# Two-layer decoder step on eight cores: windowed attention rebuilt with queries in the partitions and a true row maximum

## What is computed

```python
def sink_attention(q, k, v, mask, sinks):
    s = jnp.einsum('bnqhgd,bnkhd->bnhgqk', q, k, ...) * (SWA_HEAD_DIM ** -0.5)
    s = jnp.where(mask[None, :, None, None, :, :], s, NEG_INF)
    sink = sinks.astype(jnp.float32).reshape(SWA_KV_HEADS, SWA_GROUP)[None, None, :, :, None, None]
    m = jnp.maximum(jnp.max(s, axis=-1, keepdims=True), sink)
    p = jnp.exp(s - m)
    p = p / (jnp.sum(p, axis=-1, keepdims=True) + jnp.exp(sink - m))
    return jnp.einsum('bnhgqk,bnkhd->bnqhgd', p.astype(v.dtype), v)
```

## Time and profile before

| | us |
|---|---|
| median of 3 runs (lowest to highest) | 2911.85 (2911.38 to 2926.31) |
| span of the profiled execution, slowest core | 2913.1 |
| spans of the 8 cores | 2885.2 to 2913.1 |
| TensorE busy | 2194.7 (75%) |
| VectorE busy | 1130.9 (39%) |
| ScalarE busy | 895.0 (31%) |
| GpSimd busy (DMA issues) | 257.3 (9%) |

### The profile page before, as it was taken

The page is one execution under the profiler, slowest core; times in us unless marked ns, Lnnn a source line. Parts: engine busy times, 40 slices in busy tenths (PEclk is TensorE's granted clock), DMA queues, the critical chain, the costliest instruction groups (busy, mean ns, idle before and its releaser), DMA issues.

```text
span 2913.1 us, 36426 instructions; the slowest of 8 cores (2885.2 to 2913.1 us)
## 1 busy us (share of the span) xinstructions
PE 2194.7 (75%) x11759; PEld 1031.3 (35%) x11759; DVE 1130.9 (39%) x2050; ACT 895.0 (31%) x1678; POOL 257.3 (9%) x311
## 2 busy tenths in 40 slices
PE   4768876987789868887798689776654499762697
PEld 1323333433334343333243434333211245341353
DVE  4542127136431172265311631645345331271422
ACT  2441134114521251144211520445233221343211
POOL 0000100110001100100011001000111201000010
PEclk9889988998879999999798999898755689895698
DMA  9547881797549827974488369544787878625274
GB/s 197 81 60 101 122 125 30 102 141 149 86 60 138 130 36 108 145 152 73 73 116 129 46 102 139 100 73 77 205 292 264 235 112 127 98 32 111 43 113 97
DMA packets 293096, 336.42 MB, mean 115 GB/s; under 512 B 7184, under 2 KB 257808, under 8 KB 292752
## 3 DMA queue, kind: packets, MB, share of 16 engines
q0 software_dynamic: 256944, 272.89, 59.4%
q1 hardware_dynamic: 35968, 61.20, 6.8%
HBM read 528.55 MB, written 46.79 MB: 198 GB/s over the span
## 4 chain that ended last, share of the span: by engine, by line
PE 60%; DVE 14%; DMA 11%; issue 8%; ACT 6%; DVEq 1%; SPq 0%; ACTq 0%; POOL 0%; POOLq 0%
PE pb L415 59%; DMA wr<-w 5%; DVE arena L424 4%; DVE arena L433 4%; DMA arena<-st_in 4%; ACT arena L421 3%; DVE rstd L433 2%; ACT sq L421 1%; ACT L421 1%; PE pb L418 1%; DVE hT L427 1%; DMA xT<-xTp 1%; DVE arena L427 1%; DVE stat L594 1%; DMA wr<-wo 1%
## 5 line engine op out<-in xcount | busy, mean ns | idle before, releaser
L415 PE MATMUL pb<-hT,wr 128*128 128x512 bf16 x3776 | 911.9, 399 | 81.5 <-DVE hT L427 68.3
L415 PEld LDWEIGHTS pb<-hT,wr 128*128 128x128 bf16 x3776 | 379.4, 101 | 592.2 <-issue 202.9
L415 PE MATMUL pb<-arena,wr 128*128 128x512 bf16 (+1 forms) x2720 | 535.7, 362 | 47.3 <-DMA wr<-w 21.8
L421 ACT ACTIVATE arena<-pb 128x512 bf16<-128x512 f32 (+3 forms) x584 | 319.9, 559 | 718.1 <-PE pb L415 629.4
L415 PEld LDWEIGHTS pb<-arena,wr 128*128 128x128 bf16 x2720 | 255.6, 103 | 323.6 <-issue 84.9
L415 PE MATMUL pb<-arena 128*128 128x128 bf16 (+2 forms) x576 | 146.4, 358 | 277.8 <-DVE arena L424 151.7
L424 DVE TENSOR_TENSOR arena<-arena,pb 128x512 bf16<-128x512 f32 x220 | 133.7, 608 | 526.4 <-PE pb L415 505.3
L436 POOL DMA_DIRECT2D wr<-w x144 | 125.0, 869 | 1350.7 <-PE pb L415 1349.1
L421 ACT ACTIVATE sq<-xT 128x512 bf16<-128x512 f32 x160 | 93.2, 622 | 491.2 <-PE pb L415 335.2
L415 PE MATMUL pb<-wr,hT 128*128 128x512 bf16 x1024 | 234.1, 389 | 0.0
L424 DVE TENSOR_TENSOR xT<-pb,xT 128x512 f32<-128x512 f32 x96 | 66.4, 692 | 419.9 <-PE pb L415 419.9
(11 more groups left out here) (79 smaller groups left out, 1623.0 us busy)
## 6 DMA issues: line engine op xcount, KB each, us to landing
wr<-w POOLq DMA_DIRECT2D x112, 1024.0 KB, 12.2
arena<-st_in SPq DMA_DIRECT2D x64, 512.0 KB, 8.0
srs<-arena POOLq DMA_DIRECT2D x64, 512.0 KB, 7.9
wr<-wo POOLq DMA_DIRECT2D x30, 1024.0 KB, 9.6
wr<-wqk POOLq DMA_DIRECT2D x16, 1024.0 KB, 13.3
wr<-wv POOLq DMA_DIRECT2D x16, 1024.0 KB, 11.7
wr<-wg POOLq DMA_DIRECT2D x16, 1024.0 KB, 9.9
wr<-w POOLq DMA_DIRECT2D x16, 768.0 KB, 13.6
```

The source lines that it names most:

```text
L415: S.op("pe", lambda e: e.matmul(out, lhsT, rhs, start=start, stop=stop), r, w)
L421: S.op("act", lambda e: e.activation(out=out, in_=in_, func=func, bias=bias, scale=scale), r, w)
```

## The change

- Weights: the unit `kz` is gone. The query columns and the rows of `wo1` are reordered so that head j of key head 0 sits in partitions 0 to 63 and head j of key head 1 in 64 to 127 of one chunk. Keys are projected once into `kT1` (8 matmuls of 512 columns); values are projected directly with positions in the partitions (`pb<-wr,hT`, 4 times 8 matmuls of 128 columns) and a bias add on VectorE.
- Prompt attention runs over 16 quads a tile (block, four heads). `q_scores(i)`: for each key head a 512-column matmul of the identity with the additive mask, then four 256-column score matmuls with 64 rows; VectorE takes two row maxima (128 by 2 rows of 256) and two 128x4 operations; ScalarE four exponentials of 128x256 with a bias from memory and a row sum, and a 128x4 exponential. `q_norm(i)`: VectorE adds and inverts 128x4, GpSimd scales 4 times 128x256. `q_out(i)`: 8 transposes of the probabilities; for odd i a copy of 128x1024 from PSUM on ScalarE and one on VectorE, four matmuls of 512 columns and 64 output rows (`arena,v`), and a 128x512 copy on ScalarE.
- Samples: the cached keys and values come in two DMAs of 1 MB on GpSimd's queue, in front of the load of `kv`; keys are transposed 8 at a time into `KcT`; four quads, each with four sequences, through the same three functions.

```diff
-                plan += [("q1", 0), ("q1", 1), ("kz",), ("kv",), ("wo1", 0), ("wo1", 1)]
+                plan += [("q1", 0), ("q1", 1), ("kv",), ("wo1", 0), ("wo1", 1)]
...
+                dma("pool", Kc[:, :, :], ck.rearrange("b k c -> k b c"), [], [Kcb], "kc")
+                dma("pool", Vc[:, :, :], cv.rearrange("b k c -> k b c"), [], [Vcb], "vc")
...
+            for blk in range(nblk):
...
+                    mm(bk[:, c0:256], cx.hT[:, kc, cs], wu[:, kc, c0:256], kc == 0, kc == KC - 1, [wub, cx.hb[kc]], [bb])
...
+            if sample:
+                for g in range(2):
...
+                    act(KcT[:, g * 8:(g + 1) * 8, :], tbv.rearrange("p (b k) -> p b k", b=8), AF.Copy, [tbb], [KcTb[g]])
...
+            def q_scores(i):
...
+                                mm(bks[kvh][0][:, :], ident_bf, cb[:, CB_MPR:CB_MPR + 512], True, False, [cbb], [bks[kvh][1]])
+                    for u in range(2):
+                        for kvh in range(2):
+                            rows = slice(kvh * 64, (kvh + 1) * 64)
+                            bk, bb, _ = bks[kvh]
+                            mm(bk[:, u * 256:u * 256 + w_], qT1[rows, 2 * jp + u, qs], kT1[rows, blk * 128 + k0:blk * 128 + 256], False, u == 1,
+                               [kT1b[blk + 1], kT1b[blk], qT1b[2 * jp + u]], [bb])
+                    for kvh in range(2):
+                        bk, bb, _ = bks[kvh]
+                        rmax(st_[:, kvh * 2:kvh * 2 + 2], bk[:, :].rearrange("p (a s) -> p a s", a=2)[:, :, 0:w_], [bb], [stb_[0]])
+                stt(st_[:, 4:8], st_[:, 0:4], -0.125, nsv, ALU.mult, ALU.min, [stb_[0], nskb], [stb_[1]])
+                tt(st_[:, 8:12], skv, st_[:, 4:8], ALU.add, [spb, stb_[1]], [stb_[2]])
+                for e in range(4):
+                    S.op("act", (lambda o_, i_, b_, a_: (lambda en: en.activation(out=o_, in_=i_, func=AF.Exp, bias=b_, scale=0.125, accum_out=a_)))(
+                        s_[:, e, 0:w_], bks[e // 2][0][:, (e % 2) * 256:(e % 2) * 256 + w_], st_[:, 4 + e:5 + e], st_[:, 12 + e:13 + e]), [bks[e // 2][1], stb_[1]], [sb_[e], stb_[3]])
+                act(st_[:, 16:20], st_[:, 8:12], AF.Exp, [stb_[2]], [stb_[4]])
+            def q_norm(i):
...
+                tt(st_[:, 20:24], st_[:, 12:16], st_[:, 16:20], ALU.add, [stb_[3], stb_[4]], [stb_[5]])
+                recip(st_[:, 24:28], st_[:, 20:24], [stb_[5]], [stb_[6]])
+                for e in range(4):
+                    S.op("pool", (lambda o_, i_, c_: (lambda en: en.tensor_scalar(out=o_, in0=i_, scalar1=c_, scalar2=1.0, op0=ALU.mult, op1=ALU.mult)))(
+                        pn[i % 2][:, e, 0:w_], s_[:, e, 0:w_], st_[:, 24 + e:25 + e]), [sb_[e], stb_[6]], [pnb[i % 2][e]])
+            def q_out(i):
...
+                    if kvh == 0:
+                        act(pT[x][:, 0:nk * 512], tb[:, :].bitcast(BF16)[:, 0:nk * 512], AF.Copy, [tbb], [pTb[x]])
+                    else:
+                        S.op("dve", (lambda o_, i_: (lambda en: en.tensor_copy(out=o_, in_=i_)))(
+                            pT[x][:, 0:nk * 512], tb[:, :].bitcast(BF16)[:, 0:nk * 512]), [tbb], [pTb[x]])
...
+                        mm(ob[rows, :], v1[:, vb_, rows], pT[pts[kvh]][:, k * 512:(k + 1) * 512], k == 0, k == nk - 1,
+                           [v1b[vb_], pTb[pts[kvh]]], [obb])
+                act(oT[:, jg * 4:(jg + 1) * 4, qs], ob[:, :].rearrange("p (j c) -> p j c", j=4), AF.Copy, [obb], [oTb[jg][blk]])
+            q_scores(0)
+            q_scores(1)
+            q_norm(0)
+            for i in range(nquad):
+                if i + 2 < nquad:
+                    q_scores(i + 2)
+                if i + 1 < nquad:
+                    q_norm(i + 1)
+                q_out(i)
```

More of the change, by code:

```diff
@@ L219, in _consts @@
         blockmask[:, b, b * DS:(b + 1) * DS] = 1.0
-    cb = np.concatenate([ident, ones, onesz.reshape(128, -1), m_cur, m_prev, m_new, m_cache.reshape(128, -1),
-                         blockmask.reshape(128, -1)], axis=1).astype(np.float32)
+    kk = np.arange(256)[None, :]
+    qq = i[:, None]
+    ok = np.where(kk < 128, kk > qq, kk - 128 <= qq)
+    mpr = np.where(ok, 0.0, NEG)
+    msm = np.full((128, 512), NEG)
+    ti = (i % DS)[:, None]
+    msm[:, 0:128] = np.where(np.arange(128)[None, :] > ti, 0.0, NEG)
+    msm[:, 248:248 + DS] = np.where(np.arange(DS)[None, :] <= ti, 0.0, NEG)
+    cb = np.concatenate([ident, ones, blockmask.reshape(128, -1), mpr, mpr, msm], axis=1).astype(np.float32)
     cosT, sinT = _ref_rope()
@@ L237 @@
 CB_ONES = 128
[L238 to L244, removed]
+CB_BLK = 256
+CB_MPR = 2304
+CB_MSM = 2816
+CB_N = 3328
 SP_G = 0
 SP_BQ = 40
[L247 to L252, removed]
+SP_BK = 48
+SP_BO = 49
+SP_SINK = 57
+SP_BKV = 77
+SP_N = 77 + 256
 def build_program():
@@ L346, in build_program @@
         statb = [Buf(f"stat{i}") for i in range(4)]
[L347 to L350, removed]
+        kT1 = sb("kT1", [128, 128 + TT], BF16)
+        kT1b = [Buf(f"kT1{i}") for i in range(5)]
+        v1 = sb("v1", [128, 5, 128], BF16)
+        v1b = [Buf(f"v1{i}") for i in range(5)]
         banks = [es.enter_context(nc.psum_tensor(f"pb{i}", [128, 512], F32)) for i in range(8)]
@@ L920, in layer1 @@
[L920 to L944, removed]
@@ new lines, in layer1 @@
+            oTb = [[A.buf("oT") for _ in range(nblk)] for _ in range(2)]
+            tok = A.alloc("tok", [128, 256], F32)
+            tokb = A.buf("tok")
+            NQ = 3
+            ss = [A.alloc(f"ss{i}", [128, 4, 256], F32) for i in range(NQ)]
+            ssb = [[A.buf("ss") for _ in range(4)] for i in range(NQ)]
+            pn = [A.alloc(f"pn{i}", [128, 4, 256], BF16) for i in range(2)]
+            pnb = [[A.buf("pn") for _ in range(4)] for i in range(2)]
+            pT = [A.alloc(f"pT{i}", [128, 1024], BF16) for i in range(4)]
@@ new lines, in layer1 @@
+            wu, wub = wget(("kv",))
+            bk, bb, _ = pb()
+            for kc in range(KC):
+                mm(bk[:, :NT], wu[:, kc, 0:128], cx.hT[:, kc, :NT], kc == 0, kc == KC - 1, [wub, cx.hb[kc]], [bb])
+            act(kT1[:, 128:128 + NT], bk[:, :NT], AF.Identity, [bb, spb], [kT1b[1 + i] for i in range(nblk)], bias=sp[:, SP_BK:SP_BK + 1])
+            for blk in range(nblk):
+                cs = slice(blk * 128, (blk + 1) * 128)
+                last = sample or (tile_i == NPT - 1 and blk == nblk - 1)
+                c0 = 0 if last else 128
@@ L980, in layer1 @@
+                if not last:
+                    tt(v1[:, 1 + blk, :], bk[:, 128:256], sp[:, SP_BKV + 128:SP_BKV + 256], ALU.add, [bb, spb], [v1b[1 + blk]])
+                else:
+                    tt(tok[:, :], bk[:, 0:256], sp[:, SP_BKV:SP_BKV + 256], ALU.add, [bb, spb], [tokb])
+                    S.op("dve", lambda e: e.tensor_copy(out=v1[:, 1 + blk, :], in_=tok[:, 128:256]), [tokb], [v1b[1 + blk]])
                     if sample:
                         for b in range(NB):
[L982 removed]
```

353 lines of the change are left out of this document (131 added, 222 removed).

## The result

The changed kernel takes 2964.04 us (median of three runs, 2963.50 to 2964.24) against 2911.85: a ratio of 1.015, 95% interval 1.010 to 1.020. (The medians alone stand at 1.018; the three runs of the kernel before spread from 2911.38 to 2926.31.) The side (slower) and the outer range of the prediction, 2868 to 2992, held. The forecast, 2928, was 36 us short, and 2964 lies outside the 2905 to 2955 that were given to it as its own range. The profiled executions differ by nearly as much as the medians: spans of 2962.7 and 2913.1 us, 49.6 apart.

A forecast was written before the change was run, and what follows sets the result against it. VectorE was taken to bound prompt attention before, at 1.59 us a head pair. Prompt +41 us and samples -25 made +16 on 2912: 2928 us, own range 2905 to 2955, outer range 2868 to 2992.

The forecast's parts named there:

- The projections: Prompt key/value projection: dropping the `kz` unit saves 6.9 us a tile, key and value projection add at most 0.3.
- The chain through the odd steps: Prompt attention: ScalarE stands still between pairs of quads for value product, next scores and maxima, 5.5 us each time.
- O+S: TensorE's value product plus next scores between pairs of quads: 1.3 or 2.2 us at full clock, 2.6 taken.
- Engine by engine: Prompt attention: each engine's work per quad, every engine by itself under the 3.18 us of before.
- E: ScalarE's exponentials of one quad with their row sums: 2.25 us, range 1.65 to 2.5.
- breaks: ScalarE's pauses between pairs of quads in prompt attention: six a tile at 5.5 us, 33 us together.
- The loads behind attention: First two feed-forward loads, now queued behind 64 scalings: nothing, or 2 us a tile if cover is thin.
- The samples: Samples' layer 1: attention starts at about 2665, output projection at 2693 against 2719.76; -25 us, range -40 to -10.
- The false wait: Samples' layer 1: the key transposes' copy still waits for all output DMAs, so the earlier 23.68 us wait stays.
- short chain: Rival for prompt attention: free row sum, half-array matmuls side by side, full clock; 2870 us, chance 0.23.
- long chain: Rival for prompt attention: exponentials 2.5 us a quad, product and scores 3.8 at half clock; 2986 us, chance 0.20.
- GpSimd as the bound: Rival for prompt attention: GpSimd scalings at 1.3 us each, 5.2 a quad, set the pace; 2969 us, chance 0.12.

The follow-up runs named there:

- e_ahead: Changed kernel with a fourth score and statistics buffer pair, and scores and maxima issued one quad earlier, before the previous exponentials: profiled span 2891.9 us against 2962.7.
- e_split: Changed kernel with a fourth buffer pair, scores one quad earlier, and value product and output copy one quad later: ratio 0.980 to the kernel before.
- e_nosum: Changed kernel without the row sum of the exponentials, normalised by the sink terms alone: ratio 1.002 to the kernel before, span 2923.0 us.
- e_fill: Changed kernel with six unread 512-column matmuls added before each value product: ratio 1.011 to the kernel before, span 2946.1 us.
- e_pool2: Changed kernel with two of each quad's four scalings moved from GpSimd to VectorE: ratio 1.025 to the kernel before, span 2971.7 us.
- e_defer: Changed kernel, still three buffers, with only value product and output copy issued one quad later: ratio 1.002 to the kernel before, span 2927.0 us.
- before_ko: Kernel before the change, with the last prompt tile's two output DMAs on their own semaphore: ratio 0.997 to the unedited kernel before, span 2909.7 us.

## Why the prediction came out as it did

*The projections*: 28.88 us of matmuls in tile 0 became 22.55 (394.31 to 416.86), 29.50 in tile 3 became 22.98 (2572.02 to 2595.00): 6.3 and 6.5 less, 6.6 predicted. Right.

*The chain through the odd steps*: right in place and kind. Copy to next exponential 5.83 us, predicted 5.5; the idle row names VectorE, with product, masks and scores before it, as said. *e_ahead* and *e_split* are the proof, since they take the order away and leave the work. O+S was 2.77 for 2.6, the copy 1.01 for 1.04. From the maxima to the exponential it took 1.90 for 1.66: the two maxima are 1.49, the 128x4 operation 0.16, the rest is hand-over. (The prediction's 2.2 for O+S without overlap at the full clock is 2.0 by its own terms, 0.44 + 0.88 + 0.44 + 0.2; the 2.6 of the forecast does not rest on it.)

*Engine by engine*: this is the step that failed, in its term for the row sum. E was taken as 2.25 and is 2.69. The row sum is an instruction of its own, as the upper bound had it (0.19, against the 0.20 row it was read from), but the next exponential also starts later: start to start is 0.71 us with it and 0.39 without, so about 0.3 where 0.15 was taken. E lies outside its own range, 1.65 to 2.5; the upper bound charged for the instruction and not for the gap around it.

Against the forecast's 79 us the wide tiles took 89.2, 89.2 and 89.7. Of 10.2 us, E is 7.0 (sixteen times 0.44) and the breaks are 2.0 (six times 0.33); most of the rest lies ahead of the first copy of the probabilities, which came 15.9 us after the projection in tile 1 where 12.2 is the sum of the prediction's terms, 1.8 of the difference being E. The first exponential itself started 4.0 us after the projection for 3.2: a load of the activation table of 1.28 us stands right in front of it, which the prediction's fill does not name. In tile 0 it was 84.5 for 72: the narrower first block saved 4.7 us and not 7. That is 43.6 us over in the four tiles. The prompt part as a whole is over by 42.6 (83.6 for 41), and that these agree is chance: two tiles of the kernel before took 57.3 and 60.0 where the forecast set 60.9 for each, which adds 4.5, the output projections are longer (15.93 us for 64 matmuls in tile 0, which begins at the lower clock), and stages outside attention, with their scatter, took as much off again.

*The loads behind attention*: the feed-forward's first matmul does not wait for them, as predicted. In tile 0 they are issued at 498.07, and it waits for the norm, as before:

```profile
498.07 1.80 POOL L430 DMA_DIRECT2D wr<-w  x2
528.17 32.06 PE L409 MATMUL pb<-hT,wr 128*128 128x512 bf16 x126 [6.43 <-DVE hT L421]
```

*The samples*: -35 us where -25 was taken, within -40 to -10. The false wait stayed, as predicted (25.58 us, same name), but what stands before it was sized too long: `wkv`, the last of the 2.5 MB, was there at 2712, 12 us after the first issue at 2699.83, where I had put 25. That is 5 us a MB, below all three rates in the prediction.

```profile
2712.19 1.01 PE L409 MATMUL pb<-hTs_sb,wr 128*128 128x128 bf16 x8 [9.90 <-DMA wr<-wkv]
```

Behind the wait the prediction's arithmetic slips twice: its terms add to 24.4 us, not 26, and 2665 + 26 is 2691, not 2693. It took 29.1 us (2739.25 to 2768.30), so both slips helped by luck.

*The rivals*: the short chain needed three things. The half-array matmuls do run side by side: at the lower clock two mask matmuls, 1024 columns in all, took 1.03 us, four score matmuls, also 1024 columns, 0.61, and four products, 2048 columns, 1.16. The Trainium skill, "TensorE: Matmul & The Clock Gate", Part 3 (Packing small matmuls), says that such matmuls run at the same time, and the trace agrees. The row sum wasn't free (*e_nosum*) and the clock was at 0.6 (*e_fill*). The long chain is near in kind, 2986 us: its E of 2.5 was still below the measured one, but its O+S of 3.8 didn't come. GpSimd as the bound, 2969 us, is the nearest of all by its time, and that is chance: a scaling took 0.46 us, less than the 0.55 of the forecast and far from that rival's 1.3, and *e_pool2* rules it out.

So the mechanism, a break at every odd step, was right and is shown. The size was not: the prompt part came out 42.6 us over and the samples 10 under, and that these errors have opposite signs is luck.

## What to carry to other kernels

Sum the engines and you get what a kernel could take; follow one pair of iterations through every in-order queue and you get what it takes. Here the same operations run at 11.2 or at 6.8 us a pair of quads, by how early the scores and how late the value product is issued. Where an instruction waits for another engine, look at what is queued behind it, and ask the same again after moving it, since moving one link alone can bring the wait back one step later (*e_defer*). Small outputs of an instruction, such as a row sum, want a price that includes the time until the next one starts. And where a wait names a transfer that has nothing to do with the data, look for a shared semaphore, but expect the next wait behind it (*before_ko*).

## What the hardware showed beyond that

- An exponential with a row sum shows as two rows: 0.47 us and ACTIVATION_READ_ACCUMULATOR, 0.19, with 0.71 from start to start at 256 columns; without it 0.39 (*e_nosum*).
- VectorE copies 128x1024 of 2-byte values from PSUM in 0.69 us, ScalarE in 1.01. The prediction had allowed 1.2 for VectorE.
- VectorE scales 128x256 from SBUF in 0.42 us (0.84 for two, *e_pool2*), GpSimd in 0.46 (four in 1.84) to 0.50 (two in 1.00, *e_pool2*).
- Added matmuls that nobody reads made a kernel faster, by 20.5 us in the four attention stages of the prompt, by keeping the clock up (0.83 granted in the second stretch of *e_fill*, 0.60 in the first).
